# Taking the filling products at the stage borders out of a two-block transformer kernel

## What is computed

```python
# first block
h = rmsnorm(x); proj = h @ w_in                      # three kinds of attention
mixed = concat(rmsnorm(out_a), rmsnorm(out_b), rmsnorm(out_c))
x = x + rmsnorm(mixed @ w_out)
h = rmsnorm(x); u = causal_depthwise_conv(h @ w_up)
x = x + rmsnorm((gelu(gate) * up) @ w_down)
# second block
h = rmsnorm(x); proj = h @ w_in_2                    # gated linear attention and pooling
x = x + merged @ w_out_2
h2 = rmsnorm(x)
x = x + hier_moe(h2)                                 # top group, then 2 of 8 experts in it
return rmsnorm(x)
```

## Time and profile before

| | |
|---|---|
| median of 3 runs | 767.22 us (765.59 to 769.28) |
| the profiled execution, its own time | 766.47 us |
| its span, first to last instruction | 764.6 us |
| TensorE busy | 730.6 us (96% of the span) |
| VectorE, ScalarE, GpSimd busy | 364.9, 324.7, 80.4 us |
| mean granted TensorE clock | 0.986 of 2.4 GHz |
| HBM read | 179.91 MB |

### The profile page before, as it was taken

How to read it: one execution, slowest core, us unless ns; L and a number is a source line. 1 busy time by engine, 2 the same in 40 slices (tenths; PEclk the granted TensorE clock), 3 DMA queues, 4 the chain that set the end, 5 groups by cost and what they waited for, 6 DMA issues and landing times.

```text
span 764.6 us, 11657 instructions
## 1 busy us (share of the span) xinstructions
PE 730.6 (96%) x4424; PEld 528.9 (69%) x4424; DVE 364.9 (48%) x603; ACT 324.7 (42%) x537; POOL 80.4 (11%) x58
## 2 busy tenths in 40 slices
PE   6999999899999999979999999998999999999994
PEld 5887864789999999859989999866333333333332
DVE  3244434566656656764554546756233223333224
ACT  3143445365444455555625444343334333333333
POOL 0000000133443332310030000000000000000001
PEclk9999999999999999999999999987999999999998
DMA  8951313245555545432532455480999999999992
GB/s 356 423 188 56 111 55 129 90 168 189 197 171 197 181 173 211 166 111 86 187 115 111 165 172 201 178 321 30 423 423 420 424 423 421 424 423 421 424 422 108
DMA packets 25237, 181.48 MB, mean 237 GB/s; under 512 B 2800, under 2 KB 3056, under 8 KB 3568
## 3 DMA queue, kind: packets, MB, share of 16 engines
q1 hardware_dynamic: 25056, 180.90, 60.6%
q10 hardware_dynamic: 144, 0.07, 0.0%
HBM read 179.91 MB, written 1.05 MB: 237 GB/s over the span
## 4 chain that ended last, share of the span: by engine, by line
PE 83%; DVE 6%; DMA 4%; ACT 3%; issue 1%; POOL 1%; SPq 0%; POOLq 0%; DVEq 0%; ACTq 0%
PE psum L855 39%; PE psum L1076 13%; PE psum L1089 6%; PE psum L1098 5%; PE psum L551 4%; PE psum L649 4%; DMA HN<-units_in 3%; PE psum L559 3%; PE psum L608 2%; DVE ffn_w_low L446 2%; POOL rstd L1634 1%; PE psum L1068 1%; ACT ffn_w_high L441 1%; DVE arena L1901 1%; PE psum L617 1%
## 5 line engine op out<-in xcount | busy, mean ns | idle before, releaser
L446 DVE TENSOR_TENSOR ffn_w_low<-ring,ffn_w_high 128x2048 fp32r<-128x2048 f32 x57 | 134.7, 2363 | 121.0 <-ACT ffn_w_high L441 120.9
L441 ACT ACTIVATE ffn_w_high<-ring 128x2048 fp32r<-128x2048 f32 x57 | 109.3, 1918 | 143.3 <-PE psum L855 143.0
L855 PE MATMUL psum<-ht_high,ffn_w_high 128*128 128x256 f32 x576 | 163.8, 284 | 2.3 <-DVE ht_low L1885 1.3
L855 PE MATMUL psum<-ht_low,ffn_w_high 128*128 128x256 f32 x576 | 163.0, 283 | 0.0
L855 PE MATMUL psum<-ht_high,ffn_w_low 128*128 128x256 f32 x576 | 163.0, 283 | 0.0
L855 PEld LDWEIGHTS psum<-ht_high,ffn_w_high 128*128 128x128 f32 x576 | 110.5, 192 | 4.1 <-issue 2.1
L855 PEld LDWEIGHTS psum<-ht_low,ffn_w_high 128*128 128x128 f32 x576 | 110.5, 192 | 0.3
L855 PEld LDWEIGHTS psum<-ht_high,ffn_w_low 128*128 128x128 f32 x576 | 110.5, 192 | 0.0
L1248 ACT ACTIVATE arena<-psum 64x512 f32<-64x512 f32 (+6 forms) x96 | 42.9, 452 | 130.7 <-PE psum L1076 102.5
L2210 DVE TENSOR_TENSOR arena<-psum,arena 64x512 f32<-64x512 f32 x32 | 21.9, 684 | 126.5 <-ACT arena L1248 126.5
L1634 POOL TENSOR_TENSOR rstd<-ms,neghalf 128x1 f32<-128x1 f32 (+3 forms) x19 | 15.2, 803 | 511.7 <-DVE ms L1688 370.4
(11 more groups left out here) (307 smaller groups left out, 1108.5 us busy)
## 6 DMA issues: line engine op xcount, KB each, us to landing
ring<-units_in SPq DMA_DIRECT2D x117, 1024.0 KB, 5.0
more_units<-units_in SPq DMA_DIRECT2D x32, 1024.0 KB, 17.4
HN<-units_in SPq DMA_DIRECT2D x8, 1024.0 KB, 18.4
rows<-units_in SPq DMA_DIRECT2D x8, 1024.0 KB, 17.6
rows<-rows_in SPq DMA_DIRECT2D x1, 1688.0 KB, 12.3
arena<-bias_in SPq DMA_DIRECT2D x1, 1536.0 KB, 15.6
small<-small_in SPq DMA_DIRECT2D x1, 1232.0 KB, 25.6
const<-const_in SPq DMA_DIRECT2D x1, 1073.0 KB, 23.1
```

What stands on the lines that cost most here:

```text
L441: nc.scalar.activation(parts_slot(n)[0], w, ACT.Copy).then_inc(hi_ready, 1)
L446: nc.vector.tensor_tensor(l, ring[:, n % RING, :], h.bitcast(fp32), SUB).then_inc(lo_ready, 1)
L855: last = mm(o, l[a], r[b], start=start and (a, b) == pairs[0], stop=stop and (a, b) == pairs[-1])
```

## The change

The function `stay_busy`, the view `busy_with` that feeds it and its six calls are deleted. Every other instruction stays in its place on its engine, and every wait stays; the TensorE program is 22 products shorter.

```diff
-            busy_with = HT[:, :, :].rearrange("p a b -> p (a b)")
-
-            def stay_busy(count, bank=0, data=busy_with, n=512):
-
-                for _ in range(count):
-                    mm(psum[:, bank, 0:n], ident, data[:, 0:n], start=True, stop=True)
-
             def transposes(stage):
...
             pe.wait_ge(x_loaded, 16)
-            stay_busy(3, 4, X[:, 0, :], 256)
             transposes(0)
...
             out_quarter(3, w, 2).then_inc(unit_used, 1)
-            stay_busy(6)
             transposes(2)
...
                 ffn_down(c, U_GLA - FF_CHUNKS + c, ready=c + 1, final=c == FF_CHUNKS - 1)
-            stay_busy(7, 2)
             transposes(3)
...
-            stay_busy(2)
             transposes(4)
...
             last.then_inc(lg_done, 1)
-            stay_busy(2, 7)
             pe.wait_ge(m_ready, 1)
...
-            stay_busy(2, 7)
             pe.wait_ge(hn_lo, 1)
             pe.wait_ge(pg_ready, 1)
```

## The result

| | before | changed |
|---|---|---|
| median of 20 runs each | 767.99 us (765.27 to 769.79) | 770.71 us (768.18 to 772.96) |
| ratio, with its 95% interval | | 1.0036 (1.0024 to 1.0048) |
| span of the profiled execution | 764.6 us | 767.7 us |
| TensorE busy | 730.6 us (96%) | 714.4 us (93%) |
| mean granted TensorE clock | 0.986 | 0.972 |

The change costs 2.7 us of the median; by the interval it is 1.8 to 3.7 us. The direction was forecast, the size was not: 777 was said, with 771 to 782 as the range, and slower by over 0.5% with a chance of 0.91. The measured 0.36% falls in the case "within 0.5%", which had 0.08. In the changed kernel L524 is gone and other lines have moved up: L535 is L528, L551 is L544, L855 is L846, L1045 is L1034, L1068 is L1055.

A forecast was written before the change was run, and what follows sets the result against it. TensorE's products end to end were taken as the bound, so fills free nothing and only the clock costs: 2.65 + 2.65 + 0.95 + 1.9 + 2.25 = 10.4 us on 766.47 gives 776.9, said as 777, range 771 to 782.

The forecast's parts named there:

- The third rival: Not slower: first real products come at full clock without fills, time 766.5 or 766.0; decided at border 2; chance 0.06.
- the second: Short gaps are carried: border 2 and router keep their clock; start, border 3 and gathering pay 5.9, so 772.4; chance 0.14.
- 2.25 us a stage: Clock cost of a stage's first dense products without fills, half of 4.5 us at 1.2 GHz; from 1.7 to 3.0.
- 4.5 us: How long dense products run at 1.2 GHz before 2.4 GHz is granted, chosen from rows saying 3.4, 3.8 and 6 us.
- borders 2 and 3: Without their six and seven fills, first products start at half clock: 2.65 us at border 2, 0.95 at border 3.
- start: Without fills nothing lifts the clock before the first real products at 11.10: 0.4 + 2.25 = 2.65 us, from 1.7 to 3.9.
- The credit of 1.7 us: At border 3 the kernel before already pays 3.4 us at half clock, so 1.7 is subtracted from 2.65, leaving 0.95.
- border 4, all three pairs: Fills around the router: transposes and router cost 1.9 us, second pair (ranking products) 0, third pair (gathering, L1068) 2.25.
- the router's term: Border 4: clock falls before the router's products, 1.5 us for 20 products, 1.9 with the transposes, from 0 to 2.4.
- The gathering's 2.25: Border 4: without the third pair of fills L1068 starts at half clock, 2.25 us, from 1.7 to 3.0.
- The first rival: Cheap ramp: each dense start costs only 1.7 us, copies hide the transposes, border 3 unchanged; 6.6 us, so 773.1; chance 0.20.
- theory C: Border 4 is one piece: first pairs keep the router fast, only then can the third help the gathering; all three 2 to 3 us.

## Why the size was wrong

**What held.** The fills free nothing: the transposes still start right behind the rows (137.61 and 341.41), and no kernel with fills out was measurably faster. The third rival is refuted, by the clock of 0.50 at border 2, where it said it would decide itself, and the same clock refutes the second, which wanted border 2 to keep 2.4 GHz. The clock falls in the idle stretch, and the transposes cost their 0.4 to 0.5 us. Nothing downstream swallowed the delay of the gathering: behind it the lag stays at 2.9 to 3.1 us to the end of the span.

**The step that failed** is the price "2.25 us a stage", made of 4.5 us in which dense products run at 1.2 GHz. I started that clock at the first product. It starts at the first transpose. Over the nine borders 2 and 3 that stood without fills in five profiles with their sixteen transposes, the rise came 3.2 to 8.9 us after the first transpose and the first product 4.3 us after it. Five times the clock was back before the product, once 0.4 us late, three times 3.6 to 4.6 us late. The mean is 1.4 us of half clock, so 0.7 us lost, not 2.25. The argument for 4.5 us spoke of the work that must run before the clock rises, and I had sixteen slow transposes in the same sum, priced for their length and not counted as such work. The start goes the same way. In five profiles without its fills (those with single transposes) the clock was back between 0.5 us before and 1.9 us after the first product, 0.9 us of half clock as a mean and so 0.5 lost, and that product came at 11.6 us. In the ten profiles with the fills it came at 11.35 as a mean, because at the start the transposes were slow in part even so. Together that is 0.7 us where 2.65 was said.

**The second part of the error** is that I took the profiled kernel for one that pays nothing at border 2. In nine profiles of kernels with the fills of borders 2 and 3 the clock fell at one of these 18 borders five times, 3.4 us each, which is 0.5 us a border. The credit of 1.7 us that I gave border 3 for a fall there was due in four of the nine. So the net price of borders 2 and 3 is near 0.4 + 0.7 - 0.5 = 0.6 each, 1.2 together; measured 0.8 with an interval from -0.5 to 2.2, forecast 3.6.

Term by term, in us, measured by the kernels without the start's fills, without those of borders 2 and 3 and without those of border 4:

| | forecast | measured |
|---|---|---|
| start | 2.65 | 0.7 (-0.5 to 2.0) |
| borders 2 and 3 | 3.6 | 0.8 (-0.5 to 2.2) |
| border 4, all three pairs | 4.15 | 1.8 (0.2 to 3.5) |
| sum | 10.4 | 3.3 |

The sum of the three parts agrees with the whole change, 2.7 and 4.0 in its two measurements, though with intervals as wide as these that is weak support. At border 4 the router's term was sized about right for the products themselves: 6.0 against 4.3 us as means over profiles, 1.7, where I put 1.5 (for 20 products, which are 20 records of the trace). The gathering's 2.25 was not. I read the earlier trace rows as if the third pair always brought the clock back. It did in the profile before and in two others; in the other seven profiles with fills ahead of it the gathering took 9.2 to 9.5 us all the same, against 7.7 to 7.8. Without them it took 9.2 to 10.4 us in five profiles, so the third pair saves about 0.7 us as a mean, and 1.2 us was measured.

The rule of the Trainium skill (TensorE: Matmul & The Clock Gate, The HAM clock gate), that the ramp penalty is under 1% of a typical kernel's span, holds for what the change cost, 0.4 and 0.5%, as the prediction applied it; what all the slow stretches of a kernel cost together no run here separates. The first rival, which it spoke for, said 6.6 us and was still about twice too dear: it too started the slow clock at the first product. The same page of the Trainium skill also says (PE-mode transpose) that transposes do not count as busy for the clock as products do. The rows at 146.7 and 351.5 of the kernel with doubled transposes say otherwise for these float32 transposes, which the trace lists as MATMUL, and the measurement decides.

**What stays open.** Why the pair ahead of the gathering brings the clock back in some executions only, so why its term of 2.25 measured 1.2 (0.2 to 2.2); the trace gives no more than the rise and the fall. And whether border 4's parts overlap, as theory C has it, or the two larger single figures were high by chance.

## What to carry to other kernels

When a stretch of idle time ahead of a stage costs the clock, count from the first work of any kind behind it, transposes included, how long the slow clock lasts, and subtract what the kernel pays for the clock already. Fills in idle time are free and here worth 0.4 to 0.5%, but they don't hold the clock every time: here it fell behind them at 5 borders of 18, each time 0.1 to 0.4 us after the first product. Where the clock's falls move from one execution to the next, one profile is a sample: look at several before a term of a sum rests on a fall or a rise in it.

## What was not expected of the hardware

Sixteen float32 transposes at 1.2 GHz take 3.4 to 3.7 us in one block; at 2.4 GHz they take 1.1 us for each eight. With the slow block the clock was back ahead of the first product at five borders of nine, so the slowness partly heals itself, while behind the fast transposes, which have pauses between them, it fell at five borders of 18. That the pauses are the cause is likely and not shown. It also fell within the narrow router products of 36 columns, between 509.8 and 512.0 us in five of the seven profiles that have the pair of fills ahead of them, although TensorE's records show it busy throughout these products. Whether their width is the cause or the pauses of the transposes ahead of them no run separates.
